# Two queue orders and one early load in a one-core hybrid block kernel: filler epilogues ahead of the next main step, last tile's epilogue ahead of conditioning rows

## The chip, the cores and the metric

The program runs on 1 core of one Trainium2 chip. The metric is device microseconds of one execution. A core has TensorE (PE), VectorE (DVE), ScalarE (ACT), GpSimd (POOL) and SyncE (SP), each with its own in-order instruction list; semaphores join them. ACT and SP also issue the DMAs of this kernel.

## The reference, cut to what matters

Two transformer blocks are computed one after the other on 512 tokens of width 1024, all in float32:

```python
proj = h @ w_in                            # first block: one projection
ya = dilated_attention(...)                # softmax heads (A), 4
yb = stick_breaking_attention(...)         # 4 heads
yc = sliding_window_sink_attention(...)    # softmax heads (C), 4
yd = moba_attention(...)                   # softmax heads (D), 4
x += group_norm(concat(ya, yb, yc, yd)) @ w_out
x += memory_cross_attention(rmsnorm(x), rmsnorm(mem))   # 256 memory tokens
x += square(relu(rmsnorm(x) @ w_up)) @ w_down
# second block, two layers, with a 256-token context stream beside x:
mod = silu(c) @ ada_w + ada_b              # "conditioning": 6 x 1024 numbers, for c and for c_ctx
z = modulate(rmsnorm(x)) @ w_in2           # gate a, b, c; q, k, v; convolution; spatial gate
m = g_a * (y_a @ wa) + g_b * (y_b @ wb) + g_c * (y_c @ wc);  x += g1 * (m @ wo)
x += g2 * conv_ffn(modulate(rmsnorm(x)))
```

One stick-breaking head is `z = qk*scale; log_1m = log_sigmoid(-z)` for past keys, a reversed cumulative sum of it, `a = exp(log_sigmoid(z) + suffix)`, and `a @ v`.

## The kernel before

Activations lie feature-major in SBUF. Every float32 product is made of three fp32r products (hi*hi, hi*lo, lo*hi): `feature_tile` (L343 to L345) makes one output tile of 128 features from `kt` blocks of 128, that is 3*kt matmuls of 512 columns (the token stream, T) or of 256 columns (the context stream, TC). Weights come as slabs of 512 KB over SP's queue into a ring of five; POOL splits each into hi and lo.

The order of the work is one list, `order`, of (part, step), written when the program is built. Each engine walks the same list: PE calls `part.tensor`, ACT `part.scalar`, DVE `part.vector`. So an instruction that waits holds back everything later in the list on its engine. A product part (`Gemm`, `GemmTok`, `Branch`) has one step for each tile and, with a lag of one, one more: step i has tile i's products on PE and the *end* of tile i-1 on ACT and DVE (the epilogue, which reads the tile from PSUM and frees its bank). A tile takes the next bank of `rotation`, three banks (0, 1, 6) in the stages at hand and four in the MLP; its first matmul waits until the tile that had the bank before is freed.

`weave(main, filler)` (L243) spreads a filler, measured by its products, evenly over the steps of a main list; `pace(main, filler, cost)` (L259) spreads a filler of given cost over the products of a main list. They are used so:

- First stage: `pace` with the projection as main (15 tiles of in_qk, then 4 tiles each of values_c and values[0..2]) and as filler the conditioning rows `Ada(0)` (48 rows; each is a DMA issue on ACT, which waits until the row four before is done, and two L1851 instructions on DVE), then the context norm `n1c` and `Modulation(0)`. `Loads(softmax)` stands in the main list.
- Then 51 steps of the 12 softmax heads with context work woven in, and 21 steps of `stick`, the four stick-breaking heads, as `weave(attention, steps(c_c))`. A head is five steps: scores on PE and Abs, Exp on ACT (0), Ln on ACT and `max + add` on DVE (1), suffix sums on PE and Exp on ACT (2, 3), values on PE (4). `c_c` is a `Branch` of the context: 16 tiles, even ones a gate (24 matmuls; its end is one Tanh on ACT, L874), odd ones a branch (12 matmuls; its end is L897 and L900 on DVE). The masks of the heads (128 KB) are loaded by ACT in step 0 of `stick`, behind a wait for the last softmax head; PE waits for them.
- The memory steps: main is the group norm (`norm_group`, 18 steps), `out_proj` mixed with `norm_mem`, `keys_x`, `values_x`, `norm_cross`, `query_x`, `xatt` (16 units of cross attention, 19 steps), `split_x`, `out_x` mixed with `norm_mlp`. Filler is `b_c` (a `Branch`, "last": an odd tile's end is L897 and L902 on DVE, a Copy L878 on ACT, then L905 on DVE), `o_c` (8 tiles; an end is one L530 on DVE) and the norm `n2c`.
- The MLP, first half: `pace(up 16 tiles, down 8 tiles)` with the 48 rows of `Ada(1)` as filler. An up tile's end is Relu (L555, ACT), a product (L565, DVE), Copy (L557, ACT) and the lo part (L568, DVE); the down products read all 16.

A norm is: squares on ACT (L965), sums on PE (L953), root on ACT (L969), reciprocal on DVE (L988), spread on PE (L941), and for each of eight tiles an application (L1002, DVE), its hi part (L978 or L980, ACT) and its lo part (L1009 or L1011, DVE).

Of the kernel before, what the change touches and what calls it, by code (L numbers as in the profile page):

```python
# [13 lines left out]
P = 128  # L14
# [74 lines left out]
def program(nc, rows, w, ada_in, x_in, xc_in, mem_in, cc_in, cols_in, cst_in, rel_in, onehot_in, toe_mask_in, lam_in,  # L89
            rope_in, tri_in, flip_in, sgu_in, out):  # L90
    with ExitStack() as ctx:
# [136 lines left out]
        def place(part, i):  # L228

            if i == 0:  # L230
                part.begin()
            part.place(i)
            order.append((part, i))
# [6 lines left out]
        def steps(*parts):  # L240
            return [(part, i) for part in parts for i in range(part.steps)]

        def weave(main, filler):  # L243

            groups = [g if isinstance(g, list) else [g] for g in filler]
            size = [sum(part.size(i) for part, i in g) for g in groups]
            at_, behind = 0, 0
            for n, (part, i) in enumerate(main):
                place(part, i)
                while at_ < len(groups) and behind + size[at_] / 2 <= (n + 1) * sum(size) / len(main):  # L250
                    for step in groups[at_]:
                        place(*step)
                    behind += size[at_]
                    at_ += 1
            for g in groups[at_:]:
                for step in g:
                    place(*step)

        def pace(main, filler, cost):  # L259

            whole, length = sum(cost(*f) for f in filler), sum(part.size(i) for part, i in main)
            todo, behind, gone = list(filler), 0, 0
            for part, i in main:
                place(part, i)
                gone += part.size(i)
                while todo and behind + cost(*todo[0]) / 2 <= gone * whole / length:
                    behind += cost(*todo[0])
                    place(*todo.pop(0))
            for step in todo:
                place(*step)  # L270
# [34 lines left out]
        class Products(Part):  # L305
# [7 lines left out]

            def tensor(self, pe, _):
                self.part.tensor(pe, self.i)

        class Rotation(Part):

# [345 lines left out]
        class GatedConv(Epilogue):  # L664
# [24 lines left out]
            def sum(self, m):  # L689
                return self.sums[m % 4]  # L690
# [325 lines left out]
        class SoftmaxHeads(Part):  # L1016
# [34 lines left out]
            def finished(self):  # L1051
                return self.ev, self.ev0 + len(self.heads)
# [125 lines left out]
        class StickBreaking(Part):  # L1178
# [12 lines left out]
            def begin(self):  # L1191
# [6 lines left out]
                self.pv, self.pv0 = take("stick_values", n)  # L1198
                self.ev, self.ev0 = take("stick_out", n)

            def finished(self):
                return self.ev, self.ev0 + len(self.heads)

# [65 lines left out]
            def scalar(self, act, i):  # L1269
                if i == 0:  # L1270
                    act.wait_ge(*self.clear[0]())
                    act.dma_start(self.masks[:, :, :], tri_in).then_inc(tri_loaded, 16)
                h, step = divmod(i, 5)
                if h == len(self.heads):
                    return
                e0 = self.e0 + 9 * h
                if step == 0:
                    for p in range(3):
                        act.wait_ge(self.s, self.s0 + 3 * h + p + 1)
                        nc.scalar.activation(self.part(self.sp, p), self.psum(p), ACT.Abs).then_inc(self.e, 1)  # L1280
                    for p in range(3):
                        act.wait_ge(self.e, e0 + p + 1)
                        sp = self.part(self.sp, p)
                        nc.scalar.activation(sp, sp, ACT.Exp, scale=-1.0).then_inc(self.e, 1)
                if step == 1:
                    for p in range(3):
                        act.wait_ge(self.e, e0 + 3 + p + 1)
                        sp = self.part(self.sp, p)
                        nc.scalar.activation(sp, sp, ACT.Ln, bias=cst[:, ONE_COL:ONE_COL + 1]).then_inc(self.e, 1)
                if step in (2, 3):  # L1290
                    for p in ((0, 1), (2,))[step - 2]:
                        if h:
                            act.wait_ge(self.pv, self.pv0 + h)
                        act.wait_ge(self.su, self.su0 + 3 * h + p + 1)
                        nc.scalar.activation(self.part(self.a, p), self.psum(p), ACT.Exp).then_inc(self.w, 1)
# [771 lines left out]
        def head(qt, kt_, r, vcol, yt, yr, toe, blocks, sink=None):  # L2067
# [6 lines left out]
                  for h in range(4)]  # L2074
# [6 lines left out]
        stick = StickBreaking([head(4 + h // 2, 6 + h // 2, 64 * (h % 2), 256 + 64 * h, 2 + h // 2, 64 * (h % 2), 0,  # L2081
                                    causal) for h in range(4)],
                              zone("stick_sp", [P, 1280], 150), zone("stick_a", [P, 1280], 155),
                              zone("stick_masks", [P, 2, P], 160), clear=[softmax.finished])
        norm_group = Norm("", [y1[:, k, :] for k in range(8)], R256, hhi, hlo, lambda k: col("g_group", k), None,
                          [pb(b, T) for b in (2, 3, 4, 5)],
                          [zone(f"group{i}", [P, T], 150 + 2 * i)[:, :] for i in range(2)], lat.sq,
# [222 lines left out]
        main.insert(9, (Rotation(0, 1, 6), 0))  # L2310

        main.insert(16, (Loads(softmax, [lambda: (tables.st, 16), lambda: (sem("lam_out"), 1)]), 0))
        early = [(ada0, i) for i in range(4, ada0.steps - KT)]
        for i in range(KT):
            early += [(ada0, ada0.steps - KT + i), (n1c, i)]
# [36 lines left out]
        for t, ((first, norm, second), some) in enumerate(  # L2352
# [6 lines left out]
            mixed += ([attention.pop(0)] if tiled[t] else []) + norm[1:2] + some[1:]  # L2359
            for step in mixed:  # L2360
                place(*step)
        weave(attention, steps(c_c))
        main = steps(reload, load_mem, norm_group)
        for i in range(max(out_proj.steps, norm_mem.steps)):
            main += [(part, i) for part in (out_proj, norm_mem) if i < part.steps]
# [1 line left out]
        for i in range(out_x.steps):  # L2367
            main += [(out_x, i)] + ([(norm_mlp, i - 1)] if i else [])
        main += [(norm_mlp, i) for i in range(KT, norm_mlp.steps)]
        weave(main, steps(b_c, o_c, n2c))  # L2370
        run(Loads(spread1), spread1)
        rotate([0, 1, 6, 7])

# [256 lines left out]
```

## Time and profile before

| | |
|---|---|
| median of 3 runs | 3788.08 us (3781.09 to 3790.32) |
| profiled execution | 3797.46 us, its span 3795.6 us |
| PE busy | 3578.0 us, 94% |
| POOL, DVE, ACT busy | 53%, 42%, 25% |
| mean granted TensorE clock | 0.96 of full |

The page gives busy times, a strip of the span in 40 slices, the chain of work that ended last, and the costliest groups of instructions. A timeline row of the trace is: start and length in us, engine, line, operation, tiles; in brackets the idle time of the engine before it and who released it. A windows row is: stretch, its length, then for each engine busy us and (number of instructions), the granted TensorE clock, DMA share, GB/s.

### The profile page before, as it was taken

What the parts mean: (1) busy time and instruction counts of PE and PEld (TensorE: products, weight loads), DVE (VectorE), ACT (ScalarE), POOL (GpSimd) and SP (SyncE); (2) the same over time, 40 slices, a digit from 0 to 9 for tenths busy, and PEclk for the clock granted to TensorE, in tenths of its full rate; (3) what the DMA queues carried; (4) which work ended last, traced back from release to release, by engine and by line L of the source; (5) the groups of instructions that cost most, each with busy time, mean ns of one, the idle gap of its engine ahead of it and who ended that gap; (6) DMA issues with size and microseconds to landing.
All of it is one profiled execution on the core that took longest, in us unless ns stands there. A gap on an engine that the chain in (4) does not pass through costs nothing.

```text
span 3795.6 us, 47215 instructions
## 1 busy us (share of the span) xinstructions
PE 3578.0 (94%) x18826; PEld 2939.3 (77%) x18826; DVE 1582.2 (42%) x2738; ACT 961.5 (25%) x2038; POOL 2028.6 (53%) x1216
## 2 busy tenths in 40 slices
PE   8998989989999999899998999999998998999999
PEld 6876667877789988768776787888678776887887
DVE  7744541335853222582454213340563554214330
ACT  2135434223102111221343212220221443112210
POOL 4455353654569987644332465665544332555655
PEclk9899989988999999999999999999999999999999
DMA  7533122323654433422211232332322111232322
GB/s 294 179 125 98 59 88 93 102 78 124 226 188 141 143 130 111 158 68 73 67 51 34 73 95 83 96 93 92 109 68 73 57 55 40 81 92 83 95 86 103
DMA packets 109868, 389.26 MB, mean 103 GB/s; under 512 B 12057, under 2 KB 16537, under 8 KB 108242
## 3 DMA queue, kind: packets, MB, share of 16 engines
q1 hardware_dynamic: 89280, 315.10, 26.0%
q10 hardware_dynamic: 20370, 71.13, 5.4%
q8 instruction: 151, 2.47, 0.3%
q14 instruction: 67, 0.55, 0.0%
HBM read 379.86 MB, written 6.32 MB: 102 GB/s over the span
## 4 chain that ended last, share of the span: by engine, by line
PE 80%; DVE 12%; ACT 4%; issue 2%; DMA 1%; POOL 1%; ACTq 0%; DVEq 0%; SPq 0%
PE ps L343 20%; PE ps L345 20%; PE ps L344 20%; PE ps L1380 3%; PE ps L433 2%; PE ps L435 2%; PE ps L434 2%; PE ps L953 2%; DVE ada L1851 2%; DVE junk L1851 2%; PE ps L1392 1%; DVE ps L1002 1%; DVE small_d L1437 1%; PE ps L1094 1%; PE ps L1360 1%
## 5 line engine op out<-in xcount | busy, mean ns | idle before, releaser
L2425 POOL CAST whi<-raw 128x1024 fp32r<-128x1024 f32 (+1 forms) x606 | 619.0, 1021 | 1706.2 <-DMA raw<-in_w 1705.6
L2427 POOL TENSOR_TENSOR wlo<-raw,whi 128x1024 fp32r<-128x1024 f32 (+1 forms) x606 | 1421.5, 2346 | 48.5
L343 PE MATMUL ps<-hhi,whi 128*128 128x512 f32 x2056 | 843.1, 410 | 70.6 <-DVE hlo L1009 14.2
L344 PE MATMUL ps<-hlo,whi 128*128 128x512 f32 x2056 | 819.7, 399 | 0.0
L345 PE MATMUL ps<-hhi,wlo 128*128 128x512 f32 x2056 | 818.6, 398 | 0.0
L343 PEld LDWEIGHTS ps<-hhi,whi 128*128 128x128 f32 x2056 | 394.1, 192 | 187.8 <-DVE hlo L1009 21.2
L345 PEld LDWEIGHTS ps<-hhi,wlo 128*128 128x128 f32 x2056 | 394.8, 192 | 88.5
L344 PEld LDWEIGHTS ps<-hlo,whi 128*128 128x128 f32 x2056 | 395.6, 192 | 87.4 <-issue 6.7
L343 PE MATMUL ps<-chi,whi 128*128 128x256 f32 x864 | 254.9, 295 | 4.0 <-DVE mc_lo L905 4.0
L344 PE MATMUL ps<-clo,whi 128*128 128x256 f32 x864 | 247.9, 287 | 0.0
L345 PE MATMUL ps<-chi,wlo 128*128 128x256 f32 x864 | 247.5, 286 | 0.0
L1437 DVE TENSOR_REDUCE small_d<-ps 128x1 f32<-128x768 f32 x128 | 121.9, 953 | 198.9 <-PE ps L1380 198.9
L632 DVE RECIPROCAL ps<-ps 128x512 f32<-128x512 f32 (+1 forms) x56 | 150.0, 2679 | 72.5 <-ACT ps L612 72.4
L343 PEld LDWEIGHTS ps<-chi,whi 128*128 128x128 f32 x864 | 169.5, 196 | 12.0 <-issue 6.7
L659 DVE SCALAR_TENSOR_TENSOR f_sum<-ps,cols,f_sum 128x511 f32<-128x511 f32 x88 | 66.0, 750 | 252.7 <-ACT f_sum L704 252.7
L344 PEld LDWEIGHTS ps<-clo,whi 128*128 128x128 f32 x864 | 169.9, 197 | 0.7
L345 PEld LDWEIGHTS ps<-chi,wlo 128*128 128x128 f32 x864 | 169.2, 196 | 0.0
L433 PE MATMUL ps<-whi,hhi 128*128 128x256 f32 (+1 forms) x512 | 152.2, 297 | 17.9 <-DVE ab_lo L1800 14.2
L1420 ACT ACTIVATE diff_p<-ps 128x512 f32<-128x512 f32 (+1 forms) x128 | 62.2, 486 | 377.8 <-PE ps L1360 377.8
L530 DVE SCALAR_TENSOR_TENSOR x<-ps,mod,x 128x512 f32<-128x512 f32 x32 | 24.0, 751 | 310.1 <-PE ps L345 310.1
L435 PE MATMUL ps<-whi,hlo 128*128 128x256 f32 (+1 forms) x512 | 149.9, 293 | 0.0
L434 PE MATMUL ps<-wlo,hhi 128*128 128x256 f32 (+1 forms) x512 | 149.8, 293 | 0.0
(375 smaller groups left out, 6428.2 us busy)
## 6 DMA issues: line engine op xcount, KB each, us to landing
raw<-in_w SPq DMA_DIRECT2D x574, 512.0 KB, 3.6
ada<-in_ada ACTq DMA_DIRECT2D x96, 512.0 KB, 4.6
raw<-in_w SPq DMA_DIRECT2D x16, 384.0 KB, 3.3
att_toe<-toe_dram ACTq DMA_DIRECT2D x12, 256.0 KB, 3.2
raw<-in_w SPq DMA_DIRECT2D x16, 192.0 KB, 2.4
x<-in_x SPq DMA_DIRECT2D x4, 512.0 KB, 10.6
cond<-in_cc ACTq DMA_DIRECT2D x2, 1024.0 KB, 7.2
kc_dram<-kc ACTq DMA_DIRECT2D x2, 1024.0 KB, 3.9
```

Source lines behind the costliest of these rows:

```text
L343: nc.tensor.matmul(o, whi[:, buf, c], hi[:, k, 0:n], start=(k == 0), stop=False)
L344: nc.tensor.matmul(o, whi[:, buf, c], lo[:, k, 0:n], start=False, stop=False)
L345: mm = nc.tensor.matmul(o, wlo[:, buf, c], hi[:, k, 0:n], start=False, stop=(k == kt - 1))
L433: nc.tensor.matmul(o, self.hi[:, k, a], whi[:, s % RING, c], start=(k == 0), stop=False)
L434: nc.tensor.matmul(o, self.hi[:, k, a], wlo[:, s % RING, c], start=False, stop=False)
L435: mm = nc.tensor.matmul(o, self.lo[:, k, a], whi[:, s % RING, c], start=False, stop=(k == KT - 1))
L632: nc.vector.reciprocal(self.stats[m % 2], self.stats[m % 2]).then_inc(self.rr, 1)
L1380: mm = nc.tensor.matmul(pb(2 + 2 * a, n1 - n0, n0), self.q[r, h, b * P:(b + 1) * P], self.k[r, h, n0:n1], start=True, stop=True)
L1437: nc.vector.tensor_reduce(small[0][:, a:a + 1], pb(2 + 2 * a, TT), AX_X, ALU.max)\
L1851: nc.vector.tensor_tensor_reduce(self.ring[i % r][:, :] if c else self.junk[:, :], self.ring[i % r][:, :], ps[:, 1024 * (1 + c):1024 * (2 ...
L2425: nc.gpsimd.tensor_copy(whi[:, buf, 0:c], raw[:, buf, 0:c]).then_inc(slab_hi, 1)
L2427: nc.gpsimd.tensor_tensor(wlo[:, buf, 0:c], raw[:, buf, 0:c], whi[:, buf, 0:c].bitcast(F32), ALU.subtract).then_inc(slab_split, 1)
```

## The change

Three things are edited. (1) `weave` gets a flag `ends_first`, set for the stick-breaking weave and for the memory weave: once a filler tile's products are placed, its end is placed right behind them (`Ends`), ahead of the next main step, and the next tile is later placed with its products alone (`Opened`). The places of the products do not change. (2) `pace` places no filler between the last tile of a part and that part's last end. (3) The masks of the stick-breaking heads are loaded in the first stage, right behind `Loads(softmax)`, into a place of their own, and no longer in step 0 of `stick`.

```diff
+        def weave(main, filler, ends_first=False):
+            todo, behind, total, last = list(filler), 0, sum(part.size(i) for part, i in filler), None
+            for n, step in enumerate(main):
+                place(*step)
+                while todo and behind + todo[0][0].size(todo[0][1]) / 2 <= (n + 1) * total / len(main):
+                    part, i = todo.pop(0)
+                    behind += part.size(i)
+                    place(part, i)
+                    last = (part.part, part.i) if isinstance(part, Opened) else (part, i)
+                if ends_first and todo and (todo[0][0], todo[0][1] - 1) == last and isinstance(last[0], (Gemm, Branch)):
+                    place(Ends(*todo[0]), 0)
+                    todo[0] = Opened(*todo[0]), 0
@@ pace
-            for part, i in main:
+            for n, (part, i) in enumerate(main):
                 place(part, i)
                 gone += part.size(i)
+                if n + 1 < len(main) and main[n + 1][1] and not main[n + 1][0].size(main[n + 1][1]):
+                    continue
@@
+        class Opened(Products):
+            def size(self, _):
+                return self.part.size(self.i)
@@ StickBreaking
+            def load(self, act):
+                act.dma_start(self.masks[:, :, :], tri_in).then_inc(tri_loaded, 16)
@@ StickBreaking.scalar, i == 0
                     act.wait_ge(*self.clear[0]())
-                    act.dma_start(self.masks[:, :, :], tri_in).then_inc(tri_loaded, 16)
@@
-                              zone("stick_masks", [P, 2, P], 160), clear=[softmax.finished])
+                              zone("stick_masks", [P, 2, P], 163), clear=[softmax.finished])
@@
         main.insert(16, (Loads(softmax, [lambda: (tables.st, 16), lambda: (sem("lam_out"), 1)]), 0))
+        main.insert(17, (Loads(stick), 0))
@@
-        weave(attention, steps(c_c))
+        weave(attention, steps(c_c), True)
@@
-        weave(main, steps(b_c, o_c, n2c))
+        weave(main, steps(b_c, o_c, n2c), True)
```

## Rows read from the trace of the kernel before

**Rows 1.** The page: busy times of the engines.
```profile
PE 3578.0 (94%) x18826; PEld 2939.3 (77%) x18826; DVE 1582.2 (42%) x2738; ACT 961.5 (25%) x2038; POOL 2028.6 (53%) x1216
```

**Rows 2.** Timeline of the first stage: PE, then ACT, then DVE.
```profile
129.41 0.47 PE L433 MATMUL ps<-whi,hhi 128*128 128x128 f32 x1 [2.38 <-ACT qk L490]
171.84 0.61 PE L941 MATMUL ps<-cst,norm_fc 128*128 128x128 f32 x4
183.08 0.80 PE L1072 MATMUL ps<-att_toe,att_flip 128*128 128x128 f32 x2 [2.45 <-ACT v L490]
...
123.10 5.61 ACTq L1839 DMA_DIRECT2D ada<-in_ada  x3
...
163.34 0.16 DVE L1877 TENSOR_SCALAR mod<-mod 128x16 f32<-128x16 f32 x1
182.79 0.48 DVE L1011 SCALAR_TENSOR_TENSOR clo<-cD,mod,chi 128x256 fp32r<-128x256 f32 x1 [0.18 <-ACT chi L980]
```

**Rows 3.** Windows of the first stage: half clock, full clock.
```profile
130.00:132.00 2.00, 2.00 (x11) 2.00 (x11) 1.86 (x3) 0.58 (x2) 0.59 (x1) 0.50 0.65 229
146.00:148.00 2.00, 2.00 (x19) 2.00 (x19) 1.86 (x3) 0.50 (x2) 1.92 (x2) 1.00 0.61 152
```

**Rows 4.** Timeline around stick-breaking heads 0 and 1, PE, then ACT.
```profile
564.32 0.46 PE L1243 MATMUL ps<-stick_masks,cst 128*128 128x128 f32 x2 [4.40 <-DMA stick_masks<-in_tri]
577.33 1.14 PE L1223 MATMUL ps<-stick_sp,stick_masks 128*128 128x128 f32 x4 [0.74 <-DVE stick_sp L1306]
589.91 0.39 PE L1243 MATMUL ps<-stick_masks,cst 128*128 128x128 f32 x2
599.64 1.14 PE L1223 MATMUL ps<-stick_sp,stick_masks 128*128 128x128 f32 x4 [2.10 <-DVE stick_sp L1306]
...
596.51 1.28 ACT L1289 ACT_TABLE_LOAD   x1
597.81 1.73 ACT L1289 ACTIVATE stick_sp<-stick_sp,cst 128x512 f32<-128x512 f32 x3
```

**Rows 5.** Windows of stick-breaking heads 0 and 1.
```profile
565.00:570.00 5.00, 5.00 (x16) 3.36 (x15) 0.00 (x0) 0.98 (x2) 2.61 (x2) 0.50 0.00 0
...
600.00:605.00 5.00, 5.00 (x29) 3.89 (x28) 1.88 (x5) 2.43 (x4) 4.21 (x3) 1.00 0.09 35
```

**Rows 6.** Timeline from the last up tiles to the first down tile: DVE, then PE.
```profile
1022.72 1.21 DVE L1851 CUSTOM_DVE_ANT_0 junk<-ada,ps 128x1024 f32<-128x1024 f32 x1
1027.76 0.69 DVE L565 TENSOR_TENSOR ps<-ps,tB 128x512 f32<-128x512 f32 x1
...
1029.94 0.80 PE L343 MATMUL ps<-hid_hi,whi 128*128 128x512 f32 x1 [6.11 <-DVE hid_lo L568]
```

**Rows 7.** Windows of the first down tile: half clock, full clock.
```profile
1034.00:1036.00 2.00, 2.00 (x6) 1.61 (x5) 1.86 (x3) 0.00 (x0) 0.46 (x1) 0.50 0.98 389
1036.00:1038.00 2.00, 2.00 (x10) 1.61 (x9) 1.97 (x5) 0.00 (x0) 1.92 (x2) 1.00 0.98 399
```

**Rows 8.** Timeline of the memory steps: waits of PE.
```profile
773.03 0.49 PE L343 MATMUL ps<-chi,whi 128*128 128x256 f32 x1 [1.48 <-DVE mc_lo L905]
816.12 0.39 PE L343 MATMUL ps<-chi,whi 128*128 128x256 f32 x1 [2.48 <-DVE mc_lo L905]
844.03 0.44 PE L1082 MATMUL ps<-cst,att_p 128*128 128x128 f32 x2 [1.23 <-DVE att_p L1156]
```

**Rows 9.** Timeline of the memory steps: a square, a Tanh, an odd tile's end, an `o_c` end.
```profile
655.73 0.61 ACT L965 ACTIVATE tB<-y 128x512 f32<-128x512 f32 x1
663.81 0.37 ACT L874 ACTIVATE Gc<-ps 128x256 f32<-128x256 f32 x1
755.03 0.42 DVE L897 SCALAR_TENSOR_TENSOR ps<-Gc,ps 128x256 f32<-128x256 f32 x1
852.72 0.47 DVE L530 SCALAR_TENSOR_TENSOR xc<-ps,mod,xc 128x256 f32<-128x256 f32 x1
```

**Rows 10.** A window behind the 2.48 us wait of rows 8.
```profile
818.00:820.00 2.00, 2.00 (x11) 2.00 (x11) 0.00 (x0) 0.00 (x0) 1.40 (x1) 0.50 0.00 0
```

More of the change, by code:

```diff
@@ L241, in steps @@
             return [(part, i) for part in parts for i in range(part.steps)]
[L243 to L257, printed above, removed]
+        def weave(main, filler, ends_first=False):
[10 more added lines that the diff above has]
+                    todo[0] = Opened(*todo[0]), 0
+            for step in todo:
+                place(*step)
         def pace(main, filler, cost):
```

## Prediction

> **What bounds the kernel now.** I read the busy times first: PE works 94% of the span and no other engine is near it [rows 1]. So the time is what PE does plus what it waits, and each half-clock stretch adds to what it does. POOL and the slabs never end a wait of PE in the stages at hand. I then took the timeline of PE through the stages that the change touches and looked at the brackets: the reader is to see there who ended each wait, and in the windows behind it what clock was granted. Four places stand out.
>
> (a) First stage: PE waits 2.38 us for a bank, because the copy of projection tile 14 stands on ACT behind three DMA issues of conditioning rows that took 5.61 us [rows 2]. Behind the wait the clock is 0.50 until about 145 us (full at 146); 11 matmuls fit into 2 us there, against 19 at full clock [rows 3]. At 183.08 PE waits 2.45 us more for the last value copy [rows 2].
> (b) Stick-breaking head 0: 4.40 us for the masks' DMA [rows 4], and then half clock [rows 5].
> (c) Memory steps: 1.48 and 2.48 us at context gates, both released by the lo part of an odd `b_c` tile [rows 8]. These gates take the bank of the odd tile before, since only two tiles of `values_x` or `query_x` lie between.
> (d) First down tile: 6.11 us for the end of up tile 15, which stands on DVE behind two conditioning rows, 1022.72 to 1027.76 [rows 6], and half clock after it [rows 7].
>
> **The change part by part.** All sums are against the profiled execution, 3797.46 us, which is 9.4 us above the median of 3788.08; I carry the difference over to the median.
>
> **First stage.** By the sizes in `pace`, rows 38 and 39 go behind projection step 15, row 37 to step 13, and row 23 to step 8; each value part's last end goes ahead of what filler stood in front of it, above all n15 to n17 of the context norm at the end. The copies of tiles 13 and 14 then run at about 123.5 and 124.1, as soon as row 33 lets ACT issue at 123.10 [rows 2]. Tile 14's bank is asked for at 127.0 (129.41 - 2.38), so the 2.38 us go; tile 13's is asked for at about 124.2, which just holds. The 15.7 us at half clock shrink by 1 - 11/19 [rows 3], 6.6 us. PE then gains 9.0 us by the spread of the context norm, which stands at 171.84, and would be there at 162.8. But the conditioning rows on DVE run without a gap and do not move; the modulation ends at 163.34 + 0.16 [rows 2]. The reciprocal cannot be sooner, so the spread comes at about 163.8: 8.0 us earlier, behind a new wait of 1.0 us. DVE's chain behind it ended at 182.79 + 0.48 = 183.27 and now ends at 175.3. The last value copy no longer stands behind it: PE has finished its tile at about 172.6 (183.08 - 2.45 - 8.0) and starts the softmax heads at 173.3, and their first maximum waits only for DVE at 175.3. Term: **-9 us**. Bounds: -3 if the new wait is followed by half clock as the 2.38 us one was (three value tiles, 8.5 us at full clock, cost 6 more); -11 if DVE's chain does not hold it (PE's own 9.0 and the 2.45 us at the end).
>
> The masks' own issue adds one DMA issue of some 0.35 us to ACT, in the third of the stage where ACT waits for rows anyway: nothing. It is moved past no other DMA of SP or POOL. If that cover were gone, it would cost its 0.35 us.
>
> **Stick-breaking.** The masks are long there, so head 0 starts when PE is free, at 559.9 (564.32 - 4.40). From the start of head 1 to its suffix sums are 599.64 - 589.91 = 9.73 us [rows 4]. But the new order puts the Tanh of `c_c` tile 0 between Exp and Ln of head 0, and it waits for the tile, which PE makes after the scores. In head 1 that place was PE's last product before the 2.10 us wait, ending at 597.54, 7.6 us after the head's start; the Tanh is then done at 8.1, and the table load of Ln starts there and not at 6.6 (596.51 - 589.91) [rows 4]. Suffix sums at 559.9 + 9.7 + 1.5 = 571.1, against 577.33: -6.2. PE now waits 3.6 us in front of them. Heads 2 and 3 lose one Tanh of 0.37 us [rows 9] each from the same place (there the end is now that of an odd tile, on an idle DVE): -0.7. Head 1's Tanh falls behind Ln; its table load is then the one that the next Exp would have needed, and PE does not wait there. What is late next is the clock: 3.6 us is nearer to the 4.40 us that was followed by half clock [rows 4, 5] than to the 2.10 us that was not (1.00 in 600 to 605 [rows 5]), so I charge about 8 us at half clock, 4 us. Term: **-3 us**; bounds -7 (no fall) and 0 (a longer fall).
>
> **Up to down.** The two rows go behind the end of tile 15, whose L565 starts at 1022.8 and not at 1027.76 [rows 6]: -4.9, which leaves a wait of 1.2 us. The half clock from 1029.94 to 1036 goes (6.1 us at 6 matmuls in 2 us, against 10 to 11 [rows 7]: 2.7), since 1.2 us is less than the 2.10 us after which the clock held. The rows run beside the down tile, and PE has 12 us of other work after the last row before it asks for them. Term: **-7.6 us**; bounds -4.9 and -8.5. If that slack were gone, the two rows would come back as 5 us.
>
> **Memory steps.** What is freed: the gates at 773.03 and 816.12 find their bank, -1.5 and -2.5 [rows 8]. What is added: ACT and DVE now wait for each filler tile before they go on with the main step behind it, where they used to do that main step *during* the tile. By the sizes in `weave` the filler tiles stand where they stood. Going through all of them, with L965 at 0.61, Tanh at 0.37, an odd tile's end at four instructions like the 0.42 of L897, 1.8 us with the hand-over to ACT and back, and an `o_c` end at 0.47 [rows 9], and some 0.1 to 0.3 us for each hand-over:
> - behind group norm step 0 and cross norm step 0 (tiles 0, 10): Tanh, then square 1, then its sum: 1.2 us each, 2.4
> - behind steps 5 of the same norms (tiles 1, 11): L897, L902, Copy, square 6: 2.1 each, 4.2
> - behind memory norm step 9 (tile 7): DVE waits 2 us for the tile in the middle of the applications that `keys_x` waits for: 2.1
> - in the applications of the group norm one odd end leaves and one comes, and a table load moves: 0; in the cross norm the same, less well placed: 0.5
> - behind xatt step 5 (tile 15): the end goes ahead of the probabilities: 2.0, less most of the 1.23 us at 844.03 [rows 8], which was this end later: 1.1
> - behind xatt steps 9, 11 and 14 (`o_c` 0 to 2): 0.7 each, 2.1; behind step 17, in front of the split: 1.5; beside `out_x` (`o_c` 5, 6): 0.8 each, 1.6
> - the others are covered by an `out_proj` tile of 5.6 us or by scores: 0.
> Sum 15.5, less 4.0: **+11.5 us**. Bounds: +5 if a third of the waits hides in places that I took as exposed, and +19 if they also bring half clock.
>
> One rule of the Trainium skill bears on the two loads that move. The trace has a table load of 1.28 us, and the next ACTIVATE starts 0.02 us behind it, at 597.81 [rows 4]. The page ScalarE: Activation LUTs (What ACT_TABLE_LOAD costs) adds a drain of about 1.38 us, 2.66 us in all for a switch; by it the cross norm item would be near 2 us and not 0.5, and the sum 1.4 us slower. The row decides here.
>
> Sum: -9 - 3 - 7.6 + 11.5 = **-8.1 us**: 3789.4 for an execution like the profiled one, **3780.0** against the median. What comes between the stages (the softmax steps, the MLP) has no anchor in time, so gains pass through it.
>
> **The rivals.**
> 1. *Queues less in each other's way.* In the memory steps the waits of ACT and DVE are mostly covered, and that stage costs +4 and not +11.5. For it: its waits are each only 1 to 2 us, and DVE and ACT are idle half of the time. Against it: each of the items follows from in-order queues and the places of the tiles. Sum -16: 3772.
> 2. *The clock holds in head 0.* Suffix sums wait 3.6 us but the full clock stays: -12.1: 3776.0. Against it: the 4.40 us row.
> 3. *The conditioning rows set the first stage.* The new wait at the spread brings half clock, and the value tiles eat what was gained: that term is -3, the sum -2.1: 3786.0. For it: 2.38 us did it in the same stage.
> 4. *Slower: the memory steps lose their clock.* PE gets some nine new waits of 0.7 to 2.1 us there; 2.48 us in this stage was followed by half clock [rows 10]. Each fall of about 7 us costs 3.3 us. It decides the sign when six falls come on top (8.1 + 11.4 = 19.5 us): 3800. Against it: the same stage has such falls now, some of which would go with the two waits removed.
>
> That the change does not do what it says is no rival: the orders follow from the sizes.
>
> **How the numbers follow.** A measurement of this kernel can tell 0.3%, 11.4 us. Chances: forecast 0.45 (own range 3772 to 3788), rival 1 0.22, rival 2 0.12, rival 3 0.09, rival 4 0.12. Faster by over 0.3% (below 3776.7): rivals 1 and 2 and 0.05 of the forecast, 0.39. Slower: rival 4, 0.12. Within: 0.49. For the range I add up the bounds without taking all at once: 3766 to 3797, with about 0.1 left out on each side.
>
> **What would show it.** In the profile after: no wait near 129 and 0.50 gone from 130 to 145 us; the conditioning rows still end near 160; the softmax heads start near 174. No wait for the masks, but 3 to 4 us in front of head 0's suffix sums, with `c_c`'s first Tanh ahead of Ln. About 1.2 us in front of the last hi/lo step of the first down tile. No waits at gates released by L905, but new ones at L953 (1 to 2 us, behind filler tiles), a longer one at `keys_x`, and 0.7 to 2 us at L1082 behind filler tiles. It is wrong if those waits at L953 and L1082 are missing, if the stretch from the last softmax head to the MLP is not about 8 us longer than before, or if the softmax heads start as late as before.

## The result and the profile after

The changed kernel takes 3793.98 us (median, 3784.67 to 3803.59) against 3785.97 us for the kernel before, run beside it (3781.09 to 3794.23): ratio 1.0019, 95% interval [1.0011, 1.0027], so **+7.2 us** [4.2, 10.2] where -8.1 was forecast. That is within 0.3% and inside the range given, but on the other side of nought.

The profiled execution took 3788.75 us, its span 3786.9, mean granted clock 0.965. This is *less* than the profiled execution of before (span 3795.6, clock 0.96), so two single traces can't be compared end to end. I compare them stage by stage instead, from one matmul to the same matmul (the order on PE is the same in both), and split each stretch in two: what PE waits (length less PE busy) and the granted clock, which stretches what it does. The windows of before:

```profile
120.18:190.52 70.34, 65.07 (x459) 63.59 (x457) 51.77 (x87) 16.26 (x39) 30.39 (x19) 0.83 0.40 128
553.99:656.60 102.61, 91.61 (x538) 72.28 (x538) 19.49 (x39) 39.77 (x69) 46.45 (x28) 0.95 0.23 71
656.60:1021.11 364.51, 339.87 (x1822) 284.29 (x1822) 176.10 (x331) 92.67 (x191) 199.00 (x116) 0.90 0.41 134
1021.11:1050.02 28.91, 22.38 (x84) 17.55 (x83) 26.27 (x43) 1.79 (x3) 6.86 (x4) 0.82 0.67 220
```

and of after (stretch, its length, then PE busy first, the granted clock third from the end):

```profile
120.34:185.24 64.90, 59.96 (x458) 58.43 (x457) 51.36 (x87) 16.05 (x39) 27.31 (x17) 0.92 0.44 142
547.88:646.99 99.11, 90.14 (x539) 71.71 (x538) 19.68 (x39) 40.23 (x68) 46.47 (x28) 0.97 0.23 73
646.99:1025.54 378.55, 344.27 (x1821) 287.80 (x1822) 172.82 (x329) 92.51 (x192) 198.69 (x116) 0.90 0.38 128
1025.54:1049.14 23.60, 20.95 (x84) 16.48 (x83) 21.05 (x35) 1.68 (x3) 7.77 (x5) 0.93 0.69 241
```

The reader is to see that three stretches became shorter (end of the first stage 5.4 us, stick-breaking heads 3.5, up to down 5.3) and one longer: the memory steps, 14.0 us, of which 9.6 are waits (34.28 against 24.64) and 4.4 are the same matmuls at a lower clock (344.27 busy against 339.87). The sum is -0.2 us. The spans differ by -8.7, and nearly all of that stands behind the last stretch, where the change does nothing: 2745.6 us before, 2737.8 after, and 2741.8 to 2752.4 in the sixteen other traces. This trace of after is a fast one there. The profiled execution of before was in turn a poor one in the first stretch, at a clock of 0.83, where four other kernels with the same order there ran it at 0.87 to 0.90, in 66.4 to 68.2 us and not 70.3. Both make the change look better in this pair of traces than in the timing.

The timeline of PE after, the waits that answer to [rows 2, 4, 6, 8] (line numbers stand 9 to 12 higher than before):

```profile
132.28 0.91 PE L962 MATMUL ps<-cst,cA 128*128 128x1 f32 x4 [2.41 <-ACT cA L974]
180.66 0.46 PE L1081 MATMUL ps<-att_toe,att_flip 128*128 128x128 f32 x2 [0.97 <-ACT v L499]
...
564.93 1.22 PE L1235 MATMUL ps<-stick_sp,stick_masks 128*128 128x128 f32 x4 [3.64 <-DVE stick_sp L1317]
588.88 1.27 PE L1235 MATMUL ps<-stick_sp,stick_masks 128*128 128x128 f32 x4 [2.10 <-DVE stick_sp L1317]
...
652.02 1.05 PE L962 MATMUL ps<-cst,tB 128*128 128x1 f32 x8 [1.07 <-ACT tB L974]
664.79 1.85 PE L962 MATMUL ps<-cst,tA 128*128 128x1 f32 x8 [1.99 <-ACT tA L974]
686.53 0.50 PE L352 MATMUL ps<-hhi,whi 128*128 128x512 f32 x1 [1.71 <-DVE hlo L1018]
690.41 0.80 PE L352 MATMUL ps<-hhi,whi 128*128 128x512 f32 x1 [2.91 <-DVE hlo L1018]
725.60 0.61 PE L962 MATMUL ps<-cst,tA 128*128 128x1 f32 x4 [1.79 <-ACT tA L974]
778.08 1.05 PE L962 MATMUL ps<-cst,tB 128*128 128x1 f32 x8 [1.05 <-ACT tB L974]
790.88 1.66 PE L962 MATMUL ps<-cst,tA 128*128 128x1 f32 x8 [2.00 <-ACT tA L974]
809.92 0.50 PE L352 MATMUL ps<-hhi,whi 128*128 128x512 f32 x1 [1.37 <-DVE hlo L1018]
839.56 0.44 PE L1091 MATMUL ps<-cst,att_p 128*128 128x128 f32 x2 [1.97 <-DVE att_p L1165]
...
1028.45 0.50 PE L352 MATMUL ps<-hid_hi,whi 128*128 128x512 f32 x1 [1.59 <-DVE hid_lo L577]
1030.48 0.79 PE L352 MATMUL ps<-hid_hi,whi 128*128 128x512 f32 x1 [1.06 <-DVE hid_lo L577]
```

The waits for the bank, for the masks and for the two gates are gone, and the 6.11 us one is 1.59 and 1.06. In their place stand 2.41 us in the first stage, 3.64 us in head 0, and in the memory steps five waits of 1.05 to 2.00 us for a norm's square (L962), each behind the end of a filler tile, and 1.97 us in the cross attention. The two at 686.53 and 690.41 are not new: the same tile waited 3.84 us before, in four pieces, and waits 4.62 now.

### The profile page after: what moved, and what is told of

It reads as the page before. It is cut to its first block, busy times and chain, and to the rows that moved or that the text cites. A ratio compares the mean times of both kernels' runs of the same rounds, so it can differ in the third digit from the quotient of the medians.

```text
span 3786.9 us, 47216 instructions
## 1 busy us (share of the span) xinstructions
PE 3562.6 (94%) x18826; PEld 2927.0 (77%) x18826; DVE 1575.4 (42%) x2738; ACT 961.4 (25%) x2038; POOL 2029.7 (54%) x1216
## 4 chain that ended last, share of the span: by engine, by line
PE 80%; DVE 12%; ACT 4%; issue 2%; DMA 1%; POOL 1%; ACTq 0%; DVEq 0%; SPq 0%
PE ps L352 20%; PE ps L354 20%; PE ps L353 20%; PE ps L1391 3%; PE ps L962 2%; PE ps L442 2%; PE ps L444 2%; PE ps L443 2%; DVE ada L1862 2%; DVE junk L1862 2%; PE ps L1403 1%; DVE small_d L1448 1%; DVE ps L1011 1%; PE ps L1103 1%; PE ps L1371 1%
## 6 DMA issues: line engine op xcount, KB each, us to landing
x<-in_x SPq DMA_DIRECT2D x4, 512.0 KB, 11.7
```

## The experiments

Sixteen kernels ran. All changes are given against the kernel before, in us, from the ratio of medians times its median (3788 to 3791), with the 95% interval. The stretch lengths are those of the windows above, in the trace of each kernel.

**Each part alone.** The first four each keep one part of the change and undo the others:

```diff
 e1_masks: main.insert(17, (Loads(stick), 0)) only
 e2_pace:  the "continue" in pace only
 e3_stick: weave(attention, steps(c_c), True) only
 e4_mem:   weave(main, steps(b_c, o_c, n2c), True) only
```

> The kernel before with only the masks' load moved to the first stage. Theory (each part acts by its own stage, the memory steps eat the gains): in the stick-breaking stage the 4.40 us wait goes and the half clock behind it too, since no 3.6 us wait takes its place; start of head 0 about 4.4 us earlier, its suffix sums 7.5 us earlier; time -7 us. Rival (stages elsewhere lose clock whenever the program shifts, and that decides the median): the stick stage gains the same in the profile, but the time moves by less than half of it, or the other way.

> The kernel before with only the change in pace. Theory: first stage -5 us by the first softmax steps, with the new 2.41 us wait at the context norm's first square; up to down -5 to -6 us; together -11 us in the profile up to 1050 us, and the time -11 us. Rival: the profile up to 1050 us gains 11 us but the time does not follow, because the rest of the program loses it.

> The kernel before with the ends in front only in the stick-breaking weave; the masks still load late. Theory: head 0's suffix sums 1.5 us later (Tanh in front of Ln), heads 2 and 3 0.4 us sooner each, the wait for the masks unchanged; time +1 us. If the 3.6 us wait brings a second stretch at half clock, +4 us. Rival: time changes by more than 4 us either way with no such difference in the stick stage.

> The kernel before with the ends in front only in the memory weave. Theory: +15 us between the first group norm sum and the first down tile, as in the changed kernel (-9.6 to +5.3 us against before), time +15 us. My forecast had priced this at +11.5 us. Rival (the loss of the changed kernel lies outside this stage): time +5 us or less.

Measured: masks **-3.0** [-6.1, +0.4]; pace **-8.3** [-12.5, -4.5]; stick-breaking ends **+6.1** [3.0, 9.5]; memory ends **+17.4** [12.9, 22.0]. So two parts gain, less than I took them for, and two lose; the memory ends alone lose more than the other parts gain. The masks' stretch became 6.3 us shorter in the trace (below), and the time by less than half of the 7 expected, which is the sign of that run's rival; the interval reaches -6.1, so the two aren't told apart. Pace has its -11 inside the interval. The stick-breaking ends cost more than both expectations (+1 and +4), the memory ends about the +15 expected.

**Both halves of pace, and the parts together.** `pace` is told by its caller whether to hold filler back at a part's end:

```diff
-def pace(main, filler, cost):
+def pace(main, filler, cost, tail=False):
-                if n + 1 < len(main) and main[n + 1][1] and not main[n + 1][0].size(main[n + 1][1]):
+                if tail and n + 1 < len(main) and main[n + 1][1] and not main[n + 1][0].size(main[n + 1][1]):
```

> The change to pace in the MLP alone: the end of up tile 15 goes ahead of the last two conditioning rows; the first stage is as before. My prediction's term was -7.6 (-4.9 to -8.5). Theory: -5 to -6 us, since two waits of 1.6 and 1.1 us stand in the first down tile and not one of 1.2. In the trace the first stage keeps its 2.4 us wait for the bank at about 129 and the half clock behind it. Rival: the gain of pace is all in the first stage: 0 here.

> The change to pace in the first stage alone; the MLP keeps the 6.1 us wait in front of its first down tile. My prediction's term was -9 (-3 to -11). Theory: -3 to -5 us, since a wait of 2.4 us for the first square of the context norm, behind the issues of conditioning rows on ACT, takes the place of the 2.38 us for the bank, and the gain is in the last value tile. Rival: the wait is new but the gain holds, -8 us, and the MLP gives the small rest of the 8.3 us that pace was worth.

> The masks early and the change to pace, with no end moved in either weave. If the parts add, this is -3.0 (masks alone) and -8.3 (pace alone) = -11.3 us against the kernel before, and the best of all. Rival: the two share a gain, since each part alone sat between -4 and -8 in the profile by 200 us where neither had done anything in the trace of the masks alone (the clock's own scatter); then the sum falls short, about -7. In the trace: no wait for the masks, 2.1 us in front of the suffix sums of heads 0 and 1, 1.2 us and less in the first down tile, the two gate waits of 1.48 and 2.48 us in the memory steps still there.

> As the kernel with masks early and pace, with the ends put first in the stick-breaking weave too; only the memory weave is as before. If parts add, the stick ends cost +5.5 here as alone: -6. Rival, from the whole change's trace: with the masks early there is one wait of 3.64 us in front of head 0's suffix sums and a short stretch at half clock behind it, where the stick ends alone had two long ones (behind 4.10 and behind 3.65 us); the stage was then +2.7 us over masks alone and not +6.5, so -8.5. Both say slower than the kernel without the stick ends.

Measured: MLP half **-5.7** [-8.7, -2.3]; first-stage half **-4.2** [-9.1, +0.4]; masks and pace **-13.3** [-17.8, -9.1]; these and the stick-breaking ends **-9.1** [-12.9, -4.9]. The halves add to -9.9, for -8.3 together, and masks and pace to -11.3, for -13.3: the parts add within their intervals. The stick-breaking ends cost 4.2 us with the masks early (-9.1 against -13.3, a difference with an error of some 6 us; the stretch itself takes 99.2 us against 96.5). The last step from -9.1 to the whole change's +7.2 is the memory ends, +16.3, in line with +17.4 alone.

The stretch with the stick-breaking heads, in the traces of masks alone, stick-breaking ends alone, and masks with pace:

```profile
549.98:646.29 96.31, 88.33 (x539) 70.01 (x538) 19.50 (x39) 39.81 (x69) 46.59 (x28) 0.98 0.25 75
...
546.26:655.13 108.87, 95.81 (x538) 75.52 (x538) 19.69 (x39) 40.75 (x69) 46.49 (x28) 0.91 0.20 68
...
543.83:640.30 96.47, 88.52 (x538) 70.21 (x538) 19.48 (x39) 39.79 (x69) 46.73 (x28) 0.98 0.23 75
```

It is 102.6 us before and 102.3 to 102.9 in six other kernels that leave it alone. The masks take 6.3 us off it (3.0 of waits, the rest clock: 0.98 for 0.95). The ends alone add 6.3: 2.1 of waits (13.06 against 11.00) and 4.2 of matmuls at the lower clock.

**Which ends in the memory steps.** All on top of masks and pace (-13.3), with a condition on the tile in `weave`:

```diff
 m1_gates:   weave(main, ..., lambda part, i: part is b_c and i in (9, 13))
 m2_squares: weave(main, ..., lambda part, i: part is b_c and i in (0, 1, 10, 11))
 m3_branch:  weave(main, ..., lambda part, i: part is b_c)
 m4_stick_but_first: weave(attention, steps(c_c), lambda part, i: i > 0)
```

> Masks early, pace, no stick ends; in the memory weave the end goes first only behind b_c tiles 9 and 13, the two whose lo part the gates of tiles 10 and 14 wait for. Theory: the idea of freeing the gates is sound and its price is low when only these two ends move: the waits of 1.48 and 2.48 us go and the half clock behind the second with them, -4 to -5 us against the kernel with masks and pace alone (-13.3): -17 to -18 us against the kernel before. Rival: what is freed is waited for later (the cross attention's first units, the cross norm's lo parts), so that it stands at -13 again.

> Masks early, pace, no stick ends; in the memory weave the end goes first only behind b_c tiles 0, 1, 10 and 11, which stand in front of squares 1 and 6 of the group norm and of the cross norm. My prediction charged 1.2 + 1.2 + 2.1 + 2.1 = 6.6 us to these four, so -13.3 + 6.6 = -6.7 against the kernel before. The trace of the memory ends alone has 1.07 and 1.99 us there, twice, 6.1 us in all; theory: these waits of PE bring no half clock of their own, so -7. Rival: the half clock behind them doubles the price, and this is the place of the unforeseen cost of the memory ends: -2 or slower.

> Masks early, pace, no stick ends; in the memory weave the ends of all b_c tiles go first, those of o_c and of the norm n2c stay. I charged 5.2 us to the o_c ends (2.1 + 1.5 + 1.6). The memory ends all together cost +16 to +17.5 us. Theory: o_c took 4 of them, so this stands at -13.3 + 12 = -1. Rival: the o_c ends cost nothing (in the trace their waits are 0.5 us each and partly old ones), and this stands at +3.

> Masks early, pace, memory weave as before; in the stick-breaking weave all ends go first but the Tanh of c_c tile 0, which stays behind Ln of head 0. Theory: the 4.2 us that the stick ends cost with the masks early are that one Tanh (a wait of 3.64 us in place of 2.10, and the half clock behind it), and the rest gives the 0.3 us a head that the waits of 0.96 turned 0.69 us show: -13.3 - 0.6 = -14. Rival: heads 1 to 3 carry part of it by half clock at other places: -11.

Measured: only the gates' two ends **-19.3** [-26, -13], the two gate waits gone; that is 6 us better than masks and pace, with an error of some 8. Only the four ends at the norms' squares **-4.2** [-8.3, +0.4], so +9.1 over masks and pace. All `b_c` ends **-2.3** [-6, +2], +11.0. By the timings the `o_c` ends would be the 5 us that are left of the 16.3, but the error is as large, and the trace with all `b_c` ends has the longest memory steps of all (380.0 us, where the `o_c` ends moved too gave 377.6 and 378.6): their price isn't shown. Stick-breaking ends but the first Tanh **-11.7** [-16.7, -7.2], which tells neither of its two theories from the other; in the stretch itself the trace decides for the first: the heads take 95.7 us against 96.5 without any end moved, where the one extra Tanh brought 99.2.

The memory steps in the traces of masks and pace, of the gates' ends, of the squares' ends, and, as the two marks to read them by, of masks alone (no end moved there) and of memory ends alone (all moved):

```profile
640.30:1003.94 363.64, 339.36 (x1822) 285.06 (x1822) 173.81 (x329) 92.77 (x191) 199.28 (x116) 0.90 0.40 133
...
642.32:1001.14 358.82, 335.32 (x1822) 281.29 (x1822) 173.50 (x329) 92.90 (x191) 199.16 (x116) 0.91 0.42 135
...
633.99:1009.19 375.20, 346.12 (x1822) 290.97 (x1822) 175.76 (x329) 93.07 (x192) 199.07 (x116) 0.88 0.39 129
...
646.29:1002.72 356.43, 332.84 (x1821) 279.87 (x1822) 173.04 (x329) 92.71 (x191) 199.35 (x116) 0.92 0.42 136
...
647.68:1025.27 377.59, 344.22 (x1821) 288.46 (x1822) 173.12 (x329) 92.41 (x192) 198.55 (x116) 0.89 0.39 128
```

Eleven traces have the memory steps as before. They take 356.4 to 364.5 us there, mean 362.5, and PE is busy for 332.8 to 339.9 of them: one trace can't tell less than some 8 us in this stretch.

The four ends at the squares add 4.8 us of waits (29.08 against 24.28) and 6.8 us of busy time at a clock of 0.88: more than half of their price in that execution is clock. The rival written for this run has this right in kind, and 375.2 us lies clear of the eleven. The gates' ends make the stretch 4.8 us shorter than masks and pace, but 358.8 us lies within the eleven, and the waits are only 0.8 us fewer, since a new one stands behind the second end:

```profile
788.78 0.50 PE L352 MATMUL ps<-hhi,whi 128*128 128x512 f32 x1 [3.24 <-DVE hlo L1018]
```

This is the query's first tile, held by the last application of the cross norm, which stands on DVE behind the end of tile 13.

**The second gate's end one step later, and a candidate.** The end of tile 13 is held until the next main step, the last application of the cross norm, is placed:

```diff
                 place(*step)
+                if held:
+                    place(held.pop(), 0)
...
+                    if last[0] is b_c and last[1] == 13:
+                        held.append(Ends(*todo[0]))
+                        todo[0] = Opened(*todo[0]), 0
+                        continue
```

> As the kernel with only the two gate ends first, but the end of b_c tile 13 stands one step later, behind the last application of the cross norm. Theory: in the trace with both ends right behind their tiles, VectorE holds the last application back until tile 13 is done, and PE waits 3.24 us at the query's first tile in place of 0.42; one step later this goes and the gate still finds its bank: -2.8 us more, -22 against the kernel before. Rival: the end then holds the first copies of the query back by as much: -19 as before.

> The same and the stick-breaking ends first but the first Tanh. The waits of 0.96 us in front of the suffix sums of heads 2 and 3 become 0.69: -0.5, so -22.5 where the one without stands at -22; more than 3 us between the two would mean that the stick ends do something that their waits don't show.

Measured: **-21.2** [-26, -16], and with the stick-breaking ends but the first **-22.7** [-28, -17]: 3765.73 and 3765.55 us. Both expectations hold; the interval of the first doesn't shut out its rival (-19), and the 1.5 us between the two aren't resolved. In the traces the 3.24 us are gone and the memory steps take 349.9 and 352.2 us, less than any of the eleven, with 20.0 and 20.2 us of waits, where those have 23.6 to 28.5, and a clock of 0.93 and 0.92:

```profile
642.81:992.67 349.86, 329.89 (x1822) 276.85 (x1823) 173.73 (x329) 92.55 (x191) 199.24 (x116) 0.93 0.41 138
```

These two beat both kernels, and it is they that show that the gates were worth freeing.

**What sets the end of the first stage.** With the new and the old pace, the second reduction of the last twelve conditioning rows of `Ada(0)` runs over an eighth of its columns, which leaves out a part of the context's conditioning:

```diff
+                    w = P if c and self.n == 0 and i >= 36 else 1024
-                                                   self.ring[i % r][:, :], ps[:, 1024 * (1 + c):1024 * (2 + c)],
+                                                   self.ring[i % r][:, :w], ps[:, 1024 * (1 + c):1024 * (1 + c) + w],
```

> The pace change in the first stage alone, and the second reduction of the last twelve conditioning rows of the first block runs over 128 of its 1024 columns: part of the conditioning for the context is left out, to give VectorE some 13 us back. Theory: VectorE's rows set the end of the stage, and waits of PE there only change their place; with short rows the wait in front of the sums of the context norm's first square and the half clock behind it go, and the stage ends at PE's own work: -4.2 - 6 = -10 us or more against the kernel before, with the heads starting 6 us sooner. Rival: the wait is the place of that square behind the issues of rows, and these wait for the slots' DMA as much as for VectorE: then -4 to -6.

> The same short rows, with pace as in the kernel before. Theory: here too VectorE's rows are what the waits come from, the bank wait of 2.4 us becomes 1 us or less, and this kernel stands within 2 us of the one with short rows and the new pace: once the rows don't bind, the order of ends is worth nothing. Rival: the order is worth its 4 us by itself, since the last copies still stand behind the norm's steps: this is 4 us slower than the one with the new pace.

Measured: new pace **-3.0** [-8, +1.5], old pace **+1.1** [-3.8, +5.7]. There was no -10, so the theory of the first falls. The old pace with short rows is 4.1 us behind the new, as the rival has it, but with an error of some 7 us; that it is not within 2 isn't shown by the timing. The trace of the first, PE, and windows behind it:

```profile
127.86 0.58 PE L962 MATMUL ps<-cst,cA 128*128 128x1 f32 x4 [0.52 <-ACT cA L974]
...
129.00:130.00 1.00, 1.00 (x11) 1.00 (x11) 0.97 (x3) 0.00 (x0) 1.00 (x1) 0.99 0.83 340
130.00:131.00 1.00, 1.00 (x7) 1.00 (x7) 0.86 (x3) 0.00 (x0) 0.50 (x1) 0.50 0.24 94
...
137.00:138.00 1.00, 1.00 (x11) 1.00 (x10) 0.92 (x1) 0.73 (x2) 1.00 (x1) 1.00 0.00 0
```

With the short rows the wait in front of the first square's sum is 0.52 us. With full rows and the new order it is 2.28 to 3.07 us in nine traces, but 1.44 and 0.81 in two others, so the short rows may not be the whole reason. The clock fell to 0.50 all the same, from 130.0 to about 137. The stretch took 60.9 us against 64.4 with full rows in the kernel that it was built from; but the eleven traces with full rows and the new order go from 60.0 (masks, pace and stick-breaking ends) to 64.9, and the timing has -3.0 against -4.2. So no gain from short rows is shown. In the trace with the old pace and short rows the bank wait was still 2.37 us (128.81), as that copy stands behind rows ahead of those that were shortened, and the stretch took 66.5 us. That the order of the ends is worth something by itself is thus seen in the traces; what it would be worth if no row bound, no run shows.

## Why the prediction was wrong

The signs of the four terms were right. All four came out worse than worked out (4.8, 2.2, 1.9 and 4.8 us or more, by the timings), some 14 us in all, which turns -8 into about +6; the whole change measured +7. Two steps failed in kind: in the first stage the square behind the same rows was passed over, with the half clock that it brings, and in the memory steps the half clock behind the new waits was put at nothing. The other two terms had the mechanism and were off in size.

**First stage: -9 forecast, -4.2 measured alone.** The stretch averages 63.6 us over eleven traces with the new order (60.0 to 64.9) and 67.9 over the five with the old order and full rows: -4.3. Only 0.6 of that is waits (4.5 for 5.1 us); 3.7 are the same matmuls at a better clock (59.1 busy for 62.8). Right: the bank wait went, and the rows on DVE still end where they did (163.26 + 0.16 for 163.34 + 0.16). The step that failed is "PE then gains 9.0 us by the spread". I followed DVE's chain and passed over the squares on the way, which stand on ACT behind the issues of conditioning rows exactly as the copy of tile 14 did. ACT in the kernel after:

```profile
131.17 0.33 ACTq L1850 DMA_DIRECT2D ada<-in_ada  x1
...
131.72 0.41 ACT L974 ACTIVATE cA<-xc 128x256 f32<-128x256 f32 x1
```

PE asks for that square at 129.87 and gets its sum at 132.28: the 2.38 us at the bank [rows 2] became 2.41 us at the sum, and half clock followed again [rows 3]:

```profile
134.00:139.00 5.00, 5.00 (x25) 5.00 (x25) 4.79 (x8) 0.43 (x2) 0.00 (x0) 0.50 0.07 28
139.00:144.00 5.00, 5.00 (x31) 5.00 (x31) 4.64 (x9) 0.94 (x3) 0.67 (x1) 0.64 0.65 210
```

The prediction had the half clock from 130 to 145 us gone and the softmax heads at 174 us; it held from 132 to 142.5, and the heads start at 180.7. What is left of the gain is the last value copy (0.97 us for 2.45) and a half clock that is shorter: added up from windows of 0.5 us, it lasted 13.7 to 23.9 us in the five traces with the old order, for 23.9 in the one that I read (6.8 of them behind the last value copy, which I had not charged), and 3.4 to 10.2 us in the eleven with the new. Rival 3 had the mechanism (the rows hold PE elsewhere and bring half clock there) at -3, with the wait at the spread and not at the first square.

**Stick-breaking: -3 forecast; -0.8 by timing, -3.5 by trace.** The timing is the difference of two kernels (-9.1 with the masks and ends added to pace, -8.3 for pace alone), so its error is some 6 us and it doesn't speak against -3. The wait in front of head 0's suffix sums was forecast at 3.6 and is 3.64 us, from the Tanh ahead of the table load of Ln:

```profile
558.79 1.45 ACT L1295 ACTIVATE stick_sp<-stick_sp 128x512 f32<-128x512 f32 x3
561.40 0.38 ACT L883 ACTIVATE Gc<-ps 128x256 f32<-128x256 f32 x1 [1.17 <-PE ps L354]
561.80 1.28 ACT L1300 ACT_TABLE_LOAD   x1
563.10 1.73 ACT L1300 ACTIVATE stick_sp<-stick_sp,cst 128x512 f32<-128x512 f32 x3
```

Half clock behind it was forecast for 8 us; it held for a part of one window (0.66 in 565 to 570), about 3.4 us, so that rival 2 didn't happen either. But it also came behind the 2.10 us wait of head 1, where before had full clock [rows 5], and which I had used as the row below which the clock holds:

```profile
565.00:570.00 5.00, 5.00 (x22) 4.34 (x23) 0.56 (x1) 2.11 (x3) 3.33 (x2) 0.66 0.00 0
590.00:595.00 5.00, 5.00 (x23) 4.24 (x22) 0.48 (x2) 1.45 (x4) 3.40 (x2) 0.68 0.00 0
```

The switch of tables takes 1.30 us here, from the load's start at 561.80 to the ACTIVATE at 563.10. The Trainium skill, page ScalarE: Activation LUTs (What ACT_TABLE_LOAD costs), gives 2.66 us with a drain; this row does not show the drain, and nor do the 0.02 us between the Tanh and the load. The cross norm item, on which the two differed in the prediction, came out as the row has it: the waits of the query's first tile sum to 1.72 us (0.35 and 1.37) for 1.23 before (0.39, 0.42, 0.42), +0.5.

**Up to down: -7.6 forecast, -5.7 measured alone.** Two sizes were off. A wait of 2.65 us was left (1.59 and 1.06), not 1.2: two rows still stand in front of tile 14's end on DVE, and I had moved only tile 15's. Against that, PE waits 7.7 us there in the other traces with the old order, for 6.5 in the one I read, where PE was late itself. And the clock did not come back whole: 0.93 in the stretch after, as in most traces with the new order, where I had the half clock gone; 23.7 us against 29 to 30. In three traces with the same waits it did, 1.00 and 22.2 us.

**Memory steps: +11.5 forecast, +16.3 to +17.4 measured.** The waits at the squares are where and what was written: 1.07 and 1.99, 1.05 and 2.00 for 1.2 and 2.1; so is the one in the cross attention, 1.97 for 2.0. Not foreseen was 1.79 us at 725.60, where the memory norm's first squares stand behind a Copy of an odd tile's end; of the 2.1 us charged to `keys_x` one came (2.1 us of waits there for 1.1), and of the 5.2 charged to the `o_c` ends some 2. All told the waits grew by 9.6 us, less than 11.5. The step that failed is the one that I kept for a bound and for rival 4: the new waits bring half clock, 4.4 us in both traces with all ends moved (344.27 and 344.22 busy for 339.87), and 6.6 against the mean of the eleven traces with no end moved (337.7, none above 339.9). That gives +14 by the two traces and +15.5 by the means; the +16.3 and +17.4 by timing have both inside their intervals. So rival 4 happened, at a smaller dose than the six falls that I asked of it: since the other terms were short by 9 us, it did not need them.

That the two gates were worth freeing was right, for 4.0 us written: with the second end one step later the waits are 4.3 us fewer than in masks and pace (20.0 for 24.3) and the stretch 14 us shorter, the rest clock and scatter; the timing has -7.9, with an error of some 6.5. It took two of the 24 ends that the change moved there.

What stays open: why the half clock in the first stretch lasts 13.7 us in one trace and 23.9 in another of the same order, and where some 6 us of the +7.2 are. By the means over the traces the four stretches make about +1.5 (-4.3, -3.5, +15.5, -6.1); the timings of the parts add to +8.3 (-9.1 and +17.4).

## What to carry to other kernels

An end that is placed ahead of the next main step makes that step wait for its tile on every engine the end uses. Move only the ends whose bank or result someone waits for (the bracket on PE names it), as late as that waiter allows, and behind anything that feeds PE next: two ends placed so gave 8 us (error 6.5), all of them placed early cost 16. When a wait is taken away, follow PE to the next instruction on the same engine behind the same blocker, square by square, before counting the gain. And put a price on the half clock behind new waits of 1 to 2 us: in the memory steps 9.6 us of them came with 4.4 us of clock, and 4.8 us with 6.8. Read such a price over several traces, as the same order alone varies by 7 us there.

## What the runs showed of the chip

- The granted clock fell to 0.50 (1.2 GHz) in a stretch of 128x128 matmuls 2 us behind a wait of only 0.52 us (127.86), the only wait of PE between 118 and 140 us in that trace. In the eight traces with the masks early and the first Tanh not moved, the full clock held behind the 2.10 us wait of head 0 every time; behind the same 2.10 us in head 1 it fell in seven and held in one (squares' ends), whose order there is the same. So the length of one wait doesn't tell a fall. The Trainium skill, page TensorE: Matmul & The Clock Gate (A second HAM failure mode: psum-queue depth-cycling), tells of a clock that swings where TensorE idles shortly and often between groups of matmuls, without a long wait for a DMA; no run here shows whether such idles did it.
- The same first stretch, with the same matmuls in the same order, took 66.4 to 70.3 us from one kernel's trace to another's, with 13.7 to 23.9 us of half clock. A term of 3 us can't be read from one pair of traces there; the five traces with the old order and the eleven with the new gave it.
